# Sliding-window attention with sinks: both key tiles' scores in one row of 128 columns and a sink, one turn, 0/1 masks behind it

## The reference, cut to what matters

```python
def banded_attention(q, k, v, window, sinks=None):
    ...
    def block(args):
        blk, q_blk = args
        start = blk * Q_BLOCK
        kb = lax.dynamic_slice_in_dim(k_pad, start, span, axis=2)
        ...
        rel = qpos[:, None] - kpos[None, :]
        mask = (rel >= 0) & (rel < window) & (kpos[None, :] >= 0)
        s = jnp.einsum('bgrqd,bgkd->bgrqk', q_blk, kb).astype(jnp.float32) * scale
        ...
            s = jnp.where(mask, s, -jnp.inf)
            sink = sinks.astype(jnp.float32)[None, :, :, None, None]
            m = jnp.maximum(jnp.max(s, axis=-1, keepdims=True), sink)
            p = jnp.exp(s - m)
            p = p / (jnp.sum(p, axis=-1, keepdims=True) + jnp.exp(sink - m))
        return jnp.einsum('bgrqk,bgkd->bgrqd', p.astype(vb.dtype), vb)
```

## Time and profile before

| | us |
|---|---|
| median of 3 runs | 1613.24 |
| lowest and highest of them | 1613.09, 1613.51 |
| the profiled execution | 1612.82 |
| its span in the trace | 1610.8 |

### The profile page before, as it was taken

One profiled execution on the slowest core, in us unless ns is written; L12 is line 12 of the kernel. 1 busy time (PEld: TensorE's weight loads), 2 busy tenths in 40 slices (PEclk: granted clock), 3 DMA queues, 4 the chain that ended last, 5 costly groups with the idle time before them and its releaser, 6 DMA issues.

```text
span 1610.8 us, 20972 instructions
## 1 busy us (share of the span) xinstructions
PE 1594.6 (99%) x8030; PEld 1268.1 (79%) x8030; DVE 998.0 (62%) x1392; ACT 625.8 (39%) x1210; POOL 642.9 (40%) x422
## 2 busy tenths in 40 slices
PE   9999999999999999999999999999999999999997
PEld 7888667688888666788888888887778888888886
DVE  5999255567836687676556564457746656556444
ACT  5222334544634776543222232244644322223233
POOL 3444311054422332244444444444354444444443
PEclk9999999999999999999999999999999999999998
DMA  7223201042322000023223233223002323223231
GB/s 276 92 93 104 79 13 53 14 186 95 100 71 66 14 2 2 2 92 105 92 95 102 92 105 105 98 85 105 27 29 94 101 92 105 92 99 97 92 105 52
DMA packets 37811, 133.81 MB, mean 83 GB/s; under 512 B 4752, under 2 KB 5200, under 8 KB 37200
## 3 DMA queue, kind: packets, MB, share of 16 engines
q1 hardware_dynamic: 35840, 125.65, 23.1%
q10 hardware_dynamic: 1872, 6.82, 1.1%
HBM read 130.35 MB, written 2.10 MB: 82 GB/s over the span
## 4 chain that ended last, share of the span: by engine, by line
PE 90%; issue 3%; DVE 3%; POOL 1%; ACT 1%; DMA 0%; SPq 0%; DVEq 0%; ACTq 0%; POOLq 0%
PE ps L1698 17%; PE ps L1699 17%; PE ps L1700 17%; PE ps L2207 5%; PE ps L2209 5%; PE ps L2208 5%; PE ps L2113 4%; PE ps L2151 3%; PE ps L2133 3%; PE ps L1687 1%; DVE sb_arena L956 1%; PE ps L2121 1%; PE ps L1830 1%; PE ps L1860 1%; PE ps L1883 1%
## 5 line engine op out<-in xcount | busy, mean ns | idle before, releaser
L474 POOL TENSOR_TENSOR sb_w_lo<-sb_raw,sb_w_hi 128x1024 fp32r<-128x1024 f32 x224 | 550.9, 2460 | 779.1 <-ACT sb_w_hi L505 733.5
L1698 PE MATMUL ps<-sb_x_hi,sb_w_hi 128*128 128x512 f32 x1280 | 501.8, 392 | 1.3 <-POOL sb_w_lo L474 1.3
L1700 PE MATMUL ps<-sb_x_hi,sb_w_lo 128*128 128x512 f32 x1280 | 498.2, 389 | 0.0
L1699 PE MATMUL ps<-sb_x_lo,sb_w_hi 128*128 128x512 f32 x1280 | 498.0, 389 | 0.0
L505 ACT CAST sb_w_hi<-sb_raw 128x1024 fp32r<-128x1024 f32 x226 | 237.7, 1052 | 638.9 <-PE ps L1700 432.4
L1698 PEld LDWEIGHTS ps<-sb_x_hi,sb_w_hi 128*128 128x128 f32 x1280 | 240.3, 188 | 53.5 <-issue 2.9
L1699 PEld LDWEIGHTS ps<-sb_x_lo,sb_w_hi 128*128 128x128 f32 x1280 | 240.3, 188 | 50.6 <-issue 1.4
L1700 PEld LDWEIGHTS ps<-sb_x_hi,sb_w_lo 128*128 128x128 f32 x1280 | 240.3, 188 | 50.2
L1519 DVE TENSOR_TENSOR sb_x_lo<-sb_arena,sb_x_hi 128x512 fp32r<-128x512 f32 x44 | 98.3, 2240 | 104.5 <-ACT sb_x_hi L842 104.5
L2209 PE MATMUL ps<-sb_x_hi,sb_w_lo 128*128 128x512 f32 x336 | 130.7, 389 | 0.0
L2207 PE MATMUL ps<-sb_x_hi,sb_w_hi 128*128 128x512 f32 x336 | 130.7, 389 | 0.0
(11 more groups left out here) (333 smaller groups left out, 1981.7 us busy)
## 6 DMA issues: line engine op xcount, KB each, us to landing
sb_raw<-in_w SPq DMA_DIRECT2D x227, 512.0 KB, 3.2
sb_arena<-in_cmp_w1k ACTq DMA_DIRECT2D x1, 2048.0 KB, 11.2
sb_arena<-in_cmp_w1v ACTq DMA_DIRECT2D x1, 2048.0 KB, 15.9
out<-sb_resid SPq DMA_DIRECT2D x6, 256.0 KB, 2.5
sb_resid<-in_x SPq DMA_DIRECT2D x5, 256.0 KB, 6.6
sb_arena<-in_pool_w SPq DMA_DIRECT2D x1, 1024.0 KB, 10.6
sb_arena<-in_invc SPq DMA_DIRECT2D x1, 1024.0 KB, 12.6
sb_resid<-in_x ACTq DMA_DIRECT2D x3, 256.0 KB, 6.2
```

The lines of the kernel that those rows point to most:

```text
L474: nc.gpsimd.tensor_tensor(WL[:, w % SPL], raw[:, w % RAW], WH[:, w % SPL].bitcast(F32), ALU.subtract).then_inc(tile_split, 1)
L1698: mm(out, WH[:, s, k], XH[:, k], start=(k == 0), stop=False)
L1699: mm(out, WH[:, s, k], XL[:, k], start=False, stop=False)
L1700: ins = mm(out, WL[:, s, k], XH[:, k], start=False, stop=(k == KT - 1))
```

## The change

The two key tiles are no longer side by side in a row to the end. POOL makes a second copy of the keys, with key 0 of each tile zeroed (`KS[:, 1]`). One score product then takes 256 columns, 128 of the own tile and 128 of the tile before from the copy; no mask products are added in a full unit. The sink is added to the zeroed column, at position 128. DVE puts the columns of the tile before over those of its own tile where the own key lies ahead of the query (`copy_predicated`), and the row is then 128 mixed columns and a sink. Maxima and exponentials run over 129 columns instead of 256. Four transposes take the place of eight. Behind the turn the mixed block is parted again: it is multiplied with two 0/1 masks (`SIDE`), for half 0 by DVE straight from PSUM, for half 1 by ACT, which copies it to `PTW`, and then by POOL in a new step `sides`. `VW`'s copy without key 0 goes. Short units keep their steps.

```diff
@@ attention_out (POOL)
+                def sides(u):
+
+                    if u >= len(units) or units[u][3] == 0:
+                        return
+                    v = v0 + u
+                    pool.wait_ge(pt_a, v + 1)
+                    pool.wait_ge(o_mm, v - 1)
+                    nc.gpsimd.tensor_tensor(PT_[:, v % 2, 1].rearrange("p (s r q) -> p s r q", s=2, q=P),
+                                            PTW[v % 2].rearrange("p (r q) -> p r q", q=P).unsqueeze(1).broadcast_to([P, 2, 2, P]),
+                                            SIDE.unsqueeze(2).broadcast_to([P, 2, 2, P]), ALU.mult).then_inc(pt_p, 1)
+
+                if swa:
+                    sides(0)
+                    sides(1)
                 for u in range(groups):
+                    if swa:
+                        sides(u + 2)
...
+                if w == W0["swa"] + 6:
+                    pool.wait_ge(freed, T0["swa"] + 2)
+                    step.mark(nc.gpsimd.tensor_copy(KS[:, 1], KS[:, 0]))
+                    step.wait()
+                    nc.gpsimd.memset(KS[:, 1].rearrange("p (t k) -> p t k", k=P)[:, :, 0], 0.0).then_inc(k_cut, 1)
@@ ACT
-                    n = score_columns(i, swa)
+                    n, row = (P + 1, 2 * P) if swa else (P * (i + 1), P * (i + 1))
...
-                    nc.scalar.copy(PT_[:, v % 2, 1, 0:n], psum(7, n)).then_inc(pt_a, 1)
+                    nc.scalar.copy(PTW[v % 2] if swa and i >= 1 else PT_[:, v % 2, 1, 0:n], psum(7, n)).then_inc(pt_a, 1)
...
-            act.wait_ge(sink_ready, 1)
-            nc.scalar.activation(VW[:, :, 0:2, 0:DH], values, ACT.Copy, scale=but_first).then_inc(tok_out, 1)
@@ DVE
+                    if swa and i >= 1:
+                        nc.vector.copy_predicated(s_[:, :, :, 0:P], masks[:, 1].bitcast(mybir.dt.uint16).unsqueeze(1).unsqueeze(1)
+                                                  .broadcast_to([P, 2, 2, P]), s_[:, :, :, P:2 * P]).then_inc(picked, 1)
+                        dve.wait_ge(picked, two_tiles(v - v0))
+                    if swa:
+                        s_ = s_[:, :, :, 0:P + 1]
...
-                    nc.vector.tensor_copy(PT_[:, v % 2, 0, 0:n], psum(6, n)).then_inc(pt_d, 1)
+                    if swa and i >= 1:
+                        ins = nc.vector.tensor_tensor(PT_[:, v % 2, 0].rearrange("p (s r q) -> p s r q", s=2, q=P),
+                                                      psum(6, n).rearrange("p (r q) -> p r q", q=P).unsqueeze(1).broadcast_to([P, 2, 2, P]),
+                                                      SIDE.unsqueeze(2).broadcast_to([P, 2, 2, P]), ALU.mult)
+                    else:
+                        ins = nc.vector.tensor_copy(PT_[:, v % 2, 0, 0:n], psum(6, n))
+                    ins.then_inc(pt_d, 1)
...
-                step.mark(nc.vector.tensor_scalar(but_first, ident[:, 0:1], -1.0, 1.0, ALU.mult, ALU.add))
+                step.mark(nc.vector.tensor_scalar(SIDE[:, 1], masks[:, 0], -1.0, 1.0, ALU.mult, ALU.min))
+                step.wait()
+                step.mark(nc.vector.tensor_scalar(SIDE[:, 0], SIDE[:, 1], -1.0, 1.0, ALU.mult, ALU.add))
@@ PE
+                        pe.wait_ge(k_cut, 1)
...
-                            mm(s_[hh][:, r, to:n], QN[half, c + r, P * i:P * (i + 1)], K[half, k1 - n + to:k1], start=(r == 0), stop=False)
+                            if swa and i >= 1:
+                                keys = arena[half, at:at + 6 * P].rearrange("p (b k) -> p b k", k=3 * P)[:, :, 0:P]
+                                mm(s_[hh][:, r].rearrange("p (b k) -> p b k", k=P), q, keys, start=(r == 0), stop=False)
...
-                        if swa and i >= 1:
-                            mm(s_[hh][:, :, 1:P], identb[:], masked(2, 1), start=False, stop=False)
-                        ins = mm(s_[hh][:, :, n - P:n], identb[:], masked(1), start=False, stop=True)
+                        if not swa or i == 0:
+                            ins = mm(s_[hh][:, :, P * i:P * (i + 1)], identb[:], masks[:, 1].unsqueeze(1).broadcast_to([P, pairs, P]),
+                                     start=False, stop=True)
...
-                    pe.wait_ge(pt_a, v + 1)
+                    pe.wait_ge(*((pt_p, two_tiles(v - v0)) if swa and i >= 1 else (pt_a, v + 1)))
```

More of the change, by code:

```diff
@@ L143, in maxima_done, with two_tiles @@
     return 2 * v + 2
-def score_columns(i, swa):
-    return P * len(key_tiles(i, swa)) + (1 if swa and i == 0 else 0)
+def two_tiles(v):
+    return sum(1 for c, pairs, m, i in SWA_UNITS[:v + 1] if i >= 1)
 def key_tiles(i, swa):
@@ L277, in build @@
         PTC = [carve(o1 + 10240 + 512 * i, 4, P) for i in range(2)]
+        KEYS2 = o + 8192
+        PTW = [carve(o1 + 256 * i, 2 * P) for i in range(2)]
+        SIDE = carve(o2 + 1024, 2, P)
         assert o2 + 4416 <= NA
@@ L779, in exps @@
                             ins = nc.scalar.activation(PE_[:, v % 2, hh, n * r:n * (r + 1)],
-                                                       PS[:, 2 + 2 * (v % 2) + hh, n * r:n * (r + 1)], ACT.Exp,
+                                                       PS[:, 2 + 2 * (v % 2) + hh, row * r:row * r + n], ACT.Exp,
                                                        bias=nmr[:, v % 4, hh, r:r + 1],
@@ L2112, in score @@
                             half = slice(DH * hh, DH * hh + DH)
[L2113 to L2114 removed]
+                            q = QN[half, c + r, P * i:P * (i + 1)]
+                            if swa and i >= 1:
+                                keys = arena[half, at:at + 6 * P].rearrange("p (b k) -> p b k", k=3 * P)[:, :, 0:P]
+                                mm(s_[hh][:, r].rearrange("p (b k) -> p b k", k=P), q, keys, start=(r == 0), stop=False)
+                            else:
+                                mm(s_[hh][:, r, 0:P * (i + 1)], q, K[half, 0:P * (i + 1)], start=(r == 0), stop=False)
                     for hh in range(2):
                         if swa:
[L2117 to L2121 removed]
+                            ins = mm(s_[hh][:, :, P], oneb[:, 0:1].broadcast_to([P, P]), sink_rows[:, 8 * hh + c:8 * hh + c + pairs],
+                                     start=False, stop=(i >= 1))
+                        if not swa or i == 0:
+                            ins = mm(s_[hh][:, :, P * i:P * (i + 1)], identb[:], masks[:, 1].unsqueeze(1).broadcast_to([P, pairs, P]),
+                                     start=False, stop=True)
                     ins.then_inc(s_mm, 1)
@@ L2129, in turn @@
                             pe.wait_ge(pt_a if hh else pt_d, v)
-                        js, n = key_tiles(i, swa), score_columns(i, swa)
-                        for b in range(pairs * len(js)):
-                            at = n * (b // len(js) + 1) - P * (len(js) - b % len(js))
+                        tiles = 1 if swa else i + 1
+                        for b in range(pairs * tiles):
+                            at = (P + 1) * b if swa else P * b
                             ins = nc.tensor.transpose(PS[:, 6 + hh, P * b:P * (b + 1)], PE_[:, v % 2, hh, at:at + P], ident[:])
```

25 lines of the change are left out of this document (11 added, 14 removed).

## The result

The changed kernel takes 1618.04 us at the median of 8 executions (1616.33 to 1618.86), the kernel before 1612.95 in the same session (8 executions, 1612.28 to 1614.36): a ratio of 1.0031, with a 95% interval of 1.0022 to 1.0039. It is slower by some 5 us, 0.3%, where +3.6 was forecast; the interval leaves out 1. The profiled execution took 1616.55 us, the second shortest of the eight, with a span of 1614.7.

The account below looks back on a forecast made before the run. PE was taken as the bound before the change, then a loop of 7.14 us for two units. Stretch terms 0.5 + 0 + 1.3 - 0.2 - 0.1 + 2.1 = +3.6 us gave a median of 1616.8, range 1614.5 to 1618.5.

Parts of the forecast that it names:

- signs of being right: Next profile: full units some 3.6 us, gaps ended by `sides`, copy 0.69, `sides` 1.3, some long weight copies, late output 15.
- signs of being wrong: Next profile: outputs 2.9 us apart, PE waits ending at DVE or ACT only, or granted clock below 1.00 in units.
- to output 0: Stretch up to the first unit's output: maxima 0.19 later, then ACT's copy and `sides` ahead of PE; +0.5 us.
- The chain: Full units: loop from score over DVE, ACT and POOL's `sides` to output, 7.14 us for two units, 3.57 each.
- the copy's 0.69: DVE's predicated copy in each full unit, priced at 0.69 us, with bounds of 0.546 and 1.39.
- The tail: Outputs 13 to 15: output 15 waits for POOL's split and `sides`, 2.96 us behind output 14; stretch +2.1 us.
- the edits at nothing: DVE's mask builds, POOL's key copy and the missing `VW` copy, all in idle time or unawaited; no cost.
- Rival 4: PE pauses in every unit and drops to 1.2 GHz, 2.05 us a unit above before in twelve units: 1637; chance 0.03.
- The collisions: DVE and POOL shut each other out: 0.6 in outputs 0 to 3, half of 0.9 in 3 to 6, 0.45 in 10 to 13.
- POOL's load: POOL's work in each full unit: split 1.56 plus `sides` 1.30, 2.86 us.
- Rival 1: PE stays the bound in full units at 2.905 us each, with `sides` off the loop: 1605; chance 0.11.
- Rivals 2 and 3: 2: predicated copy 0.546, no collisions, 1613.4 to 1615, chance 0.14; 3: copy 1.39 (1620.4) or `sides` 1.8, chance 0.20.

Follow-up runs that it names:

- filled_both: Changed kernel plus nineteen filler transposes in PE's waits up to output 0 and 25 more in the last two units; 1616.20 us, 1.0017 to the kernel before.
- act_first: Changed kernel with ACT copying bank 7 of a unit ahead of the next unit's exponentials instead of behind them; 1614.53 us, 1.0013 to the kernel before.
- v_step: Changed kernel, output's wait and low-weight quarters moved, half 1 rewritten with the tiles' value difference, halving `sides`; 1608.90 us, 0.9977 to the kernel before.
- late_wait: Changed kernel with output waiting for POOL's `sides` only ahead of half 1's products; 1613.63 us, 1.0009 to the kernel before.
- no_pick: Changed kernel without the predicated copy, so the result is not the reference's; 1611.91 us, 0.9997 to the kernel before.
- no_step: Changed kernel without POOL's `sides`, so half 1 of the result is not masked; 1608.25 us, 0.9973 to the kernel before.
- late_low: Changed kernel with only half 1's products waiting for `sides`, and low-weight quarters behind units 4 to 7; 1613.67 us, 1.0007 to the kernel before.

## Why the prediction held, and where it didn't

The direction and the mechanism were right, and the time lay 1.2 us above the forecast (1618.04 against 1616.8). That it came so near is partly luck, since two errors ran against each other: the schedule alone cost 0.6 to 0.9 us less than the +3.6, and the clock, which the sum had at nothing, put 1.7 on top. The signs of being right all came, and one of the signs of being wrong as well, a granted clock below 1.00 in the units. Against the stretches of the sum, from the profiled executions (after; in the last column filled_both, which has the changed kernel's schedule at full clock):

| stretch | forecast | measured | at full clock |
|---|---|---|---|
| to output 0 | +0.5 | +0.93 | +0.83 |
| 0 to 3 | 0 | +1.03 | -0.31 |
| 3 to 6 | +1.3 | +1.15 | +1.15 |
| 6 to 10 | -0.2 | -0.27 | -0.30 |
| 10 to 13 | -0.1 | -0.64 | -0.65 |
| 13 to 15 | +2.1 | +2.00 | +2.01 |
| sum | +3.6 | +4.20 | +2.73 |

The profiled executions of after and before differ by 3.73 as a whole; the 0.5 between that and 4.20 lies outside these stretches and wasn't followed up.

**The chain and the prices.** 7.14 for two units and the copy's 0.69 held to a few hundredths, the tail to a tenth. The tail is read from PE's timeline of the starts of outputs 14 and 15, before and changed: 1190.45 - 1189.12 = 1.33 and 1194.76 - 1191.93 = 2.83, where 2.96 was taken. The delay behind output 15 was passed on as it was (1.35 us to the projection, 1.38 before), and the edits at nothing cost 0.1: the first score stands at 1130.89 instead of 1130.78.

```profile
1189.12 0.38 PE L2144 MATMUL ps<-sb_ident,sb_arena 128*128 128x128 f32 x2
...
1191.93 0.41 PE L2185 MATMUL ps<-sb_ident,sb_arena 128*128 128x128 f32 x2 [0.90 <-DVE sb_arena L1458]
...
1194.76 0.41 PE L2185 MATMUL ps<-sb_ident,sb_arena 128*128 128x128 f32 x2 [1.41 <-issue]
```

**The clock was the step that failed.** Rival 4 had it as all or nothing, 2.05 us a unit, at a chance of 0.03, and the forecast itself had no term for it. I had argued that stretches with pauses under 1 us are at full clock, and so they are: in all profiled executions outputs 6 to 13 stand at 1.00 in spite of their gaps. But I hadn't asked for places with longer pauses. There are three: ahead of output 0, three pieces of 2.5 us together, the longest 1.34; ahead of output 2, one of 1.20; and ahead of outputs 14 and 15, 0.5 to 1.4 each. The profiles show the fall at the first and the last. The length of a single pause doesn't decide it here: no profile shows a fall behind the pause ahead of output 2, and act_first's shows none behind 1.72 us ahead of unit 1's turn. These two pauses in PE's timelines, the changed kernel first:

```profile
1152.77 0.41 PE L2185 MATMUL ps<-sb_ident,sb_arena 128*128 128x128 f32 x2 [1.20 <-issue]
...
1142.79 0.44 PE L2176 MATMUL ps<-sb_ident,sb_arena 128*128 128x128 f32 x2 [1.72 <-ACT sb_arena L804]
```

The term is some 1.7 us at the median. The sentence of the Trainium skill cited there (TensorE: Matmul & The Clock Gate, "HAM oscillation — how this bites in real kernels") says that idle time between bursts can drop PE to 1.2 GHz; the traces agree, with 0.50 right behind these waits, in some executions of a program and not in others.

**To output 0** I took 0.07 from ACT's copy to `sides`. The timelines of ACT and POOL show 0.08 at the second step, but 1142.45 - 1141.66 - 0.38 = 0.41 at the first:

```profile
1141.66 0.38 ACT L816 COPY sb_arena<-ps 128x256 f32<-128x256 f32 x1
...
1142.45 1.27 POOL L429 TENSOR_TENSOR sb_arena<-sb_arena 128x512 f32<-128x512 f32 x1 [7.89 <-issue]
...
1144.18 0.38 ACT L816 COPY sb_arena<-ps 128x256 f32<-128x256 f32 x1
...
1144.64 1.27 POOL L429 TENSOR_TENSOR sb_arena<-sb_arena 128x512 f32<-128x512 f32 x1 [0.92 <-ACT sb_arena L816]
```

Every profile in which `sides` is POOL's first step in the units has 0.41 or 0.42 there. In v_step, where POOL makes the difference of the values 2.5 us earlier, the first `sides` starts 1142.38 - 1141.92 - 0.38 = 0.08 behind its copy, as ACT's and POOL's timelines show:

```profile
1141.92 0.38 ACT L819 COPY sb_arena<-ps 128x256 f32<-128x256 f32 x1
...
1142.38 0.73 POOL L429 TENSOR_TENSOR sb_arena<-sb_arena 128x256 f32<-128x256 f32 x1 [2.52 <-ACT sb_arena L819]
```

So the 0.33 us more aren't a price of the step as such, which starts in time once POOL has worked in the units; why the first is later stays open.

**The collisions** of DVE and POOL came, but cost less where I had added them: 0 to 3 and 10 to 13 are 0.3 and 0.55 below my sums at full clock. The view by line of the changed kernel (shortest, median, longest) against the earlier trace rows:

```profile
L1476 DVE COPY sb_arena<-sb_small x16: 293/295/872, 1141.2 to 1191.1; 128x256 f32<-128x256 f32 x16
...
L429 POOL TENSOR_TENSOR sb_arena<-sb_arena x12: 1264/1269/1715, 1142.5 to 1193.4; 128x512 f32<-128x512 f32 x12
```

The same copy that was never above 0.302 now takes up to 0.872, and `sides` up to 1.715 where a query piece of DVE stands against it. The longest copy, in DVE's timeline, began with a quarter on POOL (1182.52 to 1183.25 above) and ended 0.15 behind it:

```profile
1182.53 0.87 DVE L1476 COPY sb_arena<-sb_small 128x256 f32<-128x256 f32 x1
```

So the sixteen copies of before hadn't settled it. The rule of the Trainium skill (SBUF — State Buffer, "Who interferes with whom") is what these rows agree with. In time the collisions weighed less than I had put them at: the schedule alone came out at 2.73, between the 3.6 with them and the 2.1 without. In 10 to 13 the long copies fell almost wholly into time in which DVE waits. How much of them lies on the path elsewhere wasn't tried.

**POOL's load** of 2.86 left out the quarters, which the prediction itself names for 6 to 10; with their 0.72 it is 3.58. In 10 to 13 POOL really carries 3.50, next to the chain's 3.57. That the chain alone gave nearly the right number there is luck: two limits happened to lie side by side. Where a run shortened the chain and left POOL's load, going by the chain was wrong, by 0.2 to 0.3 us a unit in late_wait (part of it the halves, as above) and by 0.27 in no_pick.

**The rivals.** Rival 1, PE as the bound, is what no_step shows once `sides` is gone, and v_step comes within 4 us of its 1605. Rivals 2 and 3 fell with the copy's 0.693 and `sides`' 1.357.

## What to carry to other kernels

When a change frees the bound engine, add up a whole turn of the longest loop through all engines, and each engine's full queue in that stretch, other layers' work included; here both came to some 3.5 us a unit and ate a gain that PE's own time alone had put at 10.3. Ask also where the formerly full engine will pause: here 2.5 us of pauses ahead of output 0 cost another 1.3 to 3.1 us at half clock, and in some executions only, so that the scatter grew along with the median. Where one step on a slow engine stands in the way, rewriting the sum can be worth more than reordering the queues: with half of half 1's products free of the step, and the step halved, the units took 4.4 us less in the profiles (v_step against late_low, to the projection), against 2.8 and 2.0 of the two reorderings (act_first and late_wait against filled_both).
